# Who stores last, and when: the ends of four stages of a hybrid decoder step

## The reference, cut to what matters

```
proj = rms_norm(x) @ w_in            # columns of RWKV-7 (16 heads), then of NSA
rwkv_out = rwkv7_mix(token_shift(proj[:R_COLS]))         # head norm, bonus, gate at its end
q, cmp_kv, slc_kv, win_kv, gates = nsa_heads(proj[R_COLS:])
o_cmp, sel = cmp_attend_select(q, compress(cmp rows))    # top 16 of the 64-row blocks
o_slc = slc_attend(q, sel, slc_kv)   # the sampled tokens gather blocks from a paged cache
o_win = window_attend(q, win_kv)
x = x + concat(rwkv_out, gated sum of the three) @ w_o
x = x + (silu(h @ w_gate) * (h @ w_up)) @ w_down         # h = rms_norm(x)
return rms_norm(x), the new key and value rows, the new states
```

## Time and profile before

| | us |
|---|---|
| median of 3 runs | 3618.12 (3615.64 to 3628.66) |
| profiled execution | 3612.96 |
| its span | 3611.3 |

### The profile page before, as it was taken

One profiled execution on the slowest core, in us unless ns is written; L12 is line 12 of the kernel. 1 busy time (PEld: TensorE's weight loads), 2 busy tenths in 40 slices (PEclk: granted clock), 3 DMA queues, 4 the chain that ended last, 5 costly groups with the idle time before them and its releaser, 6 DMA issues. The chain is left out here.

```text
span 3611.3 us, 68792 instructions
## 1 busy us (share of the span) xinstructions
PE 3254.6 (90%) x28367; PEld 2980.1 (83%) x28367; DVE 1958.0 (54%) x2486; ACT 1210.8 (34%) x1824; POOL 523.4 (14%) x653
## 2 busy tenths in 40 slices
PE   6999997669977999858878978999999999999997
PEld 6999997348866778644436978999999999999997
DVE  4222221753335666326643237777777777777776
ACT  4111121532323655314412234333333333333333
POOL 2000000353433333444100000000000000000000
PEclk8999999579987999869988988999999999999999
DMA  7344431565545444355252222333333332333332
GB/s 219 107 117 116 110 102 45 185 184 140 131 122 198 186 186 151 119 144 140 54 178 62 83 69 76 106 94 100 106 94 106 96 109 89 101 109 94 106 93 96
DMA packets 491834, 426.27 MB, mean 118 GB/s; under 512 B 125749, under 2 KB 440614, under 8 KB 486942
## 3 DMA queue, kind: packets, MB, share of 16 engines
q1 hardware_dynamic: 470334, 300.38, 28.9%
q0 software_dynamic: 20736, 122.13, 9.7%
q10 hardware_dynamic: 512, 0.00, 0.0%
HBM read 382.96 MB, written 66.78 MB: 125 GB/s over the span
## 5 line engine op out<-in xcount | busy, mean ns | idle before, releaser
L2763 PE MATMUL d_ps<-f_t_hi,f_w_hi 128*128 128x260 f32 x2464 | 699.9, 284 | 39.7 <-DVE f_t_lo_r L3033 32.6
L2764 PE MATMUL d_ps<-f_t_lo_r,f_w_hi 128*128 128x260 f32 x2464 | 698.9, 284 | 0.0
L2763 PEld LDWEIGHTS d_ps<-f_t_hi,f_w_hi 128*128 128x128 f32 x2464 | 467.0, 190 | 40.5 <-issue 33.2
L2764 PEld LDWEIGHTS d_ps<-f_t_lo_r,f_w_hi 128*128 128x128 f32 x2464 | 467.4, 190 | 0.0
L2782 PE MATMUL d_ps<-f_hid_r,f_w_hi 128*128 128x260 f32 x2816 | 457.2, 283 | 0.0
L2825 ACT CAST f_w_hi<-f_raw 128x1024 fp32r<-128x1024 f32 x242 | 253.9, 1049 | 500.2 <-PE d_ps L2782 268.9
L2765 PE MATMUL d_ps<-f_t_hi,f_raw_r 128*128 128x260 f32 x1408 | 399.3, 284 | 0.0
L2782 PEld LDWEIGHTS d_ps<-f_hid_r,f_w_hi 128*128 128x128 f32 x2816 | 388.6, 188 | 0.0
L2905 DVE TENSOR_TENSOR f_raw_r<-f_raw,f_w_hi 128x1024 fp32r<-128x1024 f32 x242 | 295.9, 1223 | 50.0 <-ACT f_w_hi L2825 50.0
L53 PE MATMUL p_ps<-xh,p_w_hi 128*128 128x264 f32 (+2 forms) x1504 | 306.6, 285 | 10.6 <-DVE p_w_lo L306 10.6
L55 PE MATMUL p_ps<-xl,p_w_hi 128*128 128x264 f32 (+2 forms) x1504 | 306.1, 285 | 0.0
(11 more groups left out here) (483 smaller groups left out, 5883.1 us busy)
## 6 DMA issues: line engine op xcount, KB each, us to landing
p_w<-in_w_in SPq DMA_DIRECT2D x46, 1024.0 KB, 5.6
f_raw<-in_w_gate SPq DMA_DIRECT2D x88, 512.0 KB, 3.9
f_raw<-in_w_up SPq DMA_DIRECT2D x88, 512.0 KB, 3.9
f_raw<-in_w_down SPq DMA_DIRECT2D x66, 512.0 KB, 3.6
wo_raw<-in_w_o SPq DMA_DIRECT2D x16, 1024.0 KB, 5.4
f_sums<-in_w_down SPq DMA_DIRECT2D x22, 512.0 KB, 3.6
rk_chunks<-r_outb POOLq DMA_DIRECT2D x8, 1280.0 KB, 6.2
s_cur<-rk_chunks SPq DMA_DIRECT2D x8, 1280.0 KB, 7.2
```

Of the source, the lines that this page charges most:

```text
L2763: pe.matmul(out, w, xh, start=(m < 4 and k == 0), stop=False, skip_group_check=True)
L2764: pe.matmul(out, w, xl, start=False, stop=False, skip_group_check=True)
```

## The change

Five edits, all in what one engine issues and waits for; no arithmetic is added or removed.

1. Input projection: `store_rows` and `rows_out` move from GpSimd to SyncE. The gate rows and row block 0 are issued ahead of the weights of unit CU + 10 = 44, blocks 1 to 5 behind all weights; SyncE waits for them at the end, GpSimd for its column stores alone.
2. Head normalisation: SyncE does not wait for its eight stores; they count into a new semaphore `heads_stored`, which lives on. `mix_ahead` (GpSimd, prompt stage) and each `keep_blocks` (VectorE, compression) wait for all of them. `y_t` is allocated first of the RWKV arrays, so that it is `kc` that overlies it.
3. The second `compress_load` goes from the end of the head normalisation to the start of GpSimd's list in the compression.
4. Selection: SyncE runs `prompt_ahead` before it waits for the addresses, then stores them and waits for that store. The read of the row and the 26 gathers leave the stage; in the prompt stage SyncE gathers all four heads of token 0 too.
5. Prompt attention: the stores of quarters 2 and 3 move from GpSimd to SyncE, behind its gathers; there are four semaphores `mix_stored`, one for each quarter, and SyncE waits for all four at the end.

```diff
@@ input projection, SyncE
                 for u in range(UN):
                     s, n = u % 4, wide(u)
                     if u >= 4:
                         sp.wait_ge(lo_done, u - 3)
+                    if u == CU + 10:
+                        sp.wait_ge(row_copied, 2)
+                        store_rows(grow, g.gates, NG, gates_stored)
+                        rows_out(0)
                     sp.dma_start(w_raw[:, s, :, 0:n], w_view[:, :, cols(u)]).then_inc(loaded[s], 16)
+                for c in range(1, KU // 2):
+                    rows_out(c)
+                for b in range(2):
+                    sp.wait_ge(row_stored[b], 32 * (KU // 4))
+                sp.wait_ge(gates_stored, 32)
@@ input projection, GpSimd (store_rows and rows_out word for word to SyncE)
                 for u in range(UN):
                     columns_out(u)
-                    if u == GU + 2:
-                        pool.wait_ge(row_copied, 2)
-                        store_rows(grow, g.gates, NG, gates_stored)
-                    if u >= CU + 4 and (u - CU) % 2 == 0:
-                        rows_out((u - CU - 4) // 2)
-                rows_out(KU // 2 - 1)
                 for s in range(4):
                     pool.wait_ge(stored[s], stores_of(s, UN))
-                for b in range(2):
-                    pool.wait_ge(row_stored[b], 32 * (KU // 4))
-                pool.wait_ge(gates_stored, 32)
@@ head normalisation, SyncE, then GpSimd
                 for q in range(NPAIR):
                     sp.wait_ge(out_ready, q + 1)
-                    sp.dma_start(g.mix_t[q * P:(q + 1) * P, :], g.y_t[:, q, :]).then_inc(stored, 16)
-                sp.wait_ge(stored, 16 * NPAIR)
+                    sp.dma_start(g.mix_t[q * P:(q + 1) * P, :], g.y_t[:, q, :]).then_inc(g.heads_stored, 16)
...
                 pool.wait_ge(idx_ready, 1)
-                for h in range(2):
-                    compress_load(pool, g, h, h, h + 1)
+                compress_load(pool, g, 0, 0, 1)
@@ compression, GpSimd, then VectorE
+                compress_load(pool, g, 1, 1, 2)
                 arrange(0, 0, start=True)
                 refill(0, 0)
                 arrange(0, 1)
...
                 def keep_blocks(i):
                     dve.wait_ge(fin_done, i * F2 + 1)
+                    dve.wait_ge(g.heads_stored, 16 * NPAIR)
@@ selection, SyncE
-                with nc.allow_non_contiguous_dma(reason="small tables"):
-                    sp.wait_ge(adr_ready, 1)
-                    sp.dma_start(g.adr_d, adr[:]).then_inc(adr_out, 16)
-                    sp.wait_ge(adr_out, 16)
-                    sp.dma_start(adr_row[:].rearrange("o (m k) -> o m k", k=NS),
-                                 g.adr_d.rearrange("(m f) k -> f m k", f=4)[0:1]).then_inc(adr_in, 16)
-                sp.wait_ge(adr_in, 16)
                 prompt_ahead(sp, nc, g)
-                gather(sp, g, adr_row, regs, 0, (0, 1))
+                sp.wait_ge(adr_ready, 1)
+                sp.dma_start(g.adr_d, adr[:]).then_inc(adr_out, 16)
+                sp.wait_ge(adr_out, 16)
@@ prompt attention
-        mix_stored = [sem(f"mix_stored{s}") for s in range(2)]
+        mix_stored = [sem(f"mix_stored{i}") for i in range(4)]
...
+        def store(eng, i):
+            eng.wait_ge(o_kept, 4 * i + 4)
+            eng.dma_start(g.mix_t[D_R + i * 256:D_R + i * 256 + 256, 0:SEQ].rearrange("(g d) t -> d g t", d=C),
+                           mo[half(i), :, :]).then_inc(mix_stored[i], 16)
@@ prompt attention, SyncE, then GpSimd, then VectorE
-                gather(sp, g, adr_row, regs, 0, (2, 3))
-                for b in range(1, SP_TOKENS):
+                for b in range(SP_TOKENS):
                     if b == 3:
                         wo_ahead(sp, g)
                     gather(sp, g, adr_row, regs, b, range(4))
+                store(sp, 2)
+                store(sp, 3)
+                for i in range(4):
+                    sp.wait_ge(mix_stored[i], 16)
...
-                store(0)
+                store(pool, 0)
                 gather(pool, g, late_row, regs, SP_TOKENS + 2, range(2))
-                store(1)
+                store(pool, 1)
                 gather(pool, g, late_row, regs, SP_TOKENS + 2, range(2, 4))
-                store(2)
-                store(3)
-                for s in range(2):
-                    pool.wait_ge(mix_stored[s], 32)
...
                     if i >= 2 and t == 0:
-                        dve.wait_ge(mix_stored[i % 2], 16)
+                        dve.wait_ge(mix_stored[i - 2], 16)
@@ mix_ahead, called by GpSimd in the prompt stage
 def mix_ahead(pool, g):
+    pool.wait_ge(g.heads_stored, 16 * NPAIR)
     for q in range(4):
         mix_load(pool, g, q)
```

More of the change, by code:

```diff
@@ L335, in _, with store_rows, rows_out @@
             def _(sp):
+                def store_rows(src, dst, n, sem_):
+                    sp.dma_start(dst[0:SEQ].rearrange("(t p) n -> p t n", p=P), src[:, 0:4, 0:n]).then_inc(sem_, 16)
+                    sp.dma_start(dst[SEQ:TC], src[0:NB, 4, 0:n]).then_inc(sem_, 16)
+                def rows_out(c):
+                    sp.wait_ge(row_copied, 2 * c + 3)
+                    store_rows(orow[:, c % 2], g.kv_rows[:, c * 256:(c + 1) * 256], 256, row_stored[c % 2])
                 for u in range(UN):
@@ L399, in _ @@
             def _(pool):
-                def store_rows(src, dst, n, sem_):
-                    pool.dma_start(dst[0:SEQ].rearrange("(t p) n -> p t n", p=P), src[:, 0:4, 0:n]).then_inc(sem_, 16)
-                    pool.dma_start(dst[SEQ:TC], src[0:NB, 4, 0:n]).then_inc(sem_, 16)
                 def columns_out(u):
@@ L411, in columns_out @@
                         pool.dma_start(g.k_t[r:r + P, :], ob[:, s, 0:SEQ]).then_inc(stored[s], 16)
-                def rows_out(c):
-                    pool.wait_ge(row_copied, 2 * c + 3)
-                    store_rows(orow[:, c % 2], g.kv_rows[:, c * 256:(c + 1) * 256], 256, row_stored[c % 2])
                 for u in range(UN):
                     columns_out(u)
-                    if u == GU + 2:
-                        pool.wait_ge(row_copied, 2)
-                        store_rows(grow, g.gates, NG, gates_stored)
-                    if u >= CU + 4 and (u - CU) % 2 == 0:
-                        rows_out((u - CU - 4) // 2)
-                rows_out(KU // 2 - 1)
                 for s in range(4):
                     pool.wait_ge(stored[s], stores_of(s, UN))
-                for b in range(2):
-                    pool.wait_ge(row_stored[b], 32 * (KU // 4))
-                pool.wait_ge(gates_stored, 32)
 class Arrays:
@@ L1187, in stage_rwkv_post @@
             "bonus_ready", "rec_ready", "spread_done", "spread_read"))
-        chain, out_ready, stored = new_sem(nc, g, "e_chain"), new_sem(nc, g, "e_out_ready"), new_sem(nc, g, "e_stored")
+        chain, out_ready = new_sem(nc, g, "e_chain"), new_sem(nc, g, "e_out_ready")
         iota_ready, idx_ready = new_sem(nc, g, "e_iota_ready"), new_sem(nc, g, "e_idx_ready")
@@ L1721, in stage_nsa_select @@
         adr = sb("adr", [P, NS], I32)
-        adr_row = sb("adr_row", [1, NB * 4 * NS], I32)
         pt_row = sb("pt_row", [1, NB, 2], I32)
@@ L2233, in _ @@
                 pool.tensor_copy(causal_r[:], causal[:]).then_inc(masks_ready, 1)
-                def store(i):
-                    pool.wait_ge(o_kept, 4 * i + 4)
-                    pool.dma_start(g.mix_t[D_R + i * 256:D_R + i * 256 + 256, 0:SEQ].rearrange("(g d) t -> d g t", d=C),
-                                   mo[half(i), :, :]).then_inc(mix_stored[i % 2], 16)
                 clear_old(pool, g)
@@ L3278, in compress_ahead @@
     g.m_pt_in, g.m_w_in, g.m_idc_ready = (nc.alloc_semaphore("m_" + n) for n in ("pt_in", "w_in", "idc_ready"))
+    g.heads_stored = nc.alloc_semaphore("heads_stored")
     g.b_q_in = nc.alloc_semaphore("b_q_in")
@@ L3286, in sb @@
             return ctx.enter_context(nc.sbuf_tensor(name, shape, F32))
+        g.y_t = sb("y_t", [P, NPAIR, TC])
         g.gate_t = sb("gate_t", [P, NPAIR, TC])
         g.bonus_t = sb("bonus_t", [P, NPAIR, TC])
-        g.y_t = sb("y_t", [P, NPAIR, TC])
         g.chunk_decay = sb("chunk_decay", [P, NPAIR, SEQ // C])
```

## The result

The changed kernel took **3576.66 us** (median of 4 runs, 3572.64 to 3580.08) against 3617.16 (4 runs) for the kernel before: ratio 0.9881, 95% interval 0.9857 to 0.9905, so it is faster by about 1.2%. (A ratio here is worked out from all runs of a group; the two medians alone lie 40.5 us apart.) The forecast was 3578. The profiled execution took 3572.64 us, its span 3571.0.

A forecast was written before the change was run, and what follows sets the result against it. TensorE is busy for most of the span, but stage ends wait 51 us behind VectorE without arithmetic. Gains 4.7 + 7.5 + 2.4 + 14.9 + 10.3 = 39.8 us; 3618.12 - 39.8 = 3578 us, range 3567 to 3592.

The forecast's parts named there:

- The ends of the stages: Four stages end earlier: input projection by 4.7 us, head normalisation 7.5, selection 14.9, prompt attention 10.3.
- GpSimd's drain in the projection: Input projection: begins at the key store of unit 44, two units before the end, and is over before VectorE.
- the prediction's second part: End of the input projection: with SyncE storing rows, 617.1 against 621.8, gain 4.7 us, bounds 4 to 6.5.
- The drain behind one gather: End of head normalisation: GpSimd's drain takes half of 24.3 us, over by about 1083, so not late next.
- The start of the compression: Compression's start with the second gather ahead of the first copy: gain 2.4 us, bounds a loss of 2.2 and 4.
- The replay: Compression's start, one instruction at a time from the new barrier: first copy 3.8 to 7.4, ScalarE at 8.5 instead of 10.9.
- both 64x8 casts should pass between the copies: Compression's start: VectorE's two small casts get in between GpSimd's two copies, as in the preparation stage; ScalarE starts at 8.5.
- By that rule: Compression's start under a strict port lock: second cast waits 3.6 us more, ScalarE at 11.5, sum 36.8 instead of 39.8.
- The moved gather did not block GpSimd: Rival, compression's start: GpSimd's next copy waits for the gather's descriptors; 11.8 us lost, 3590; 8%.
- The drains went with GpSimd's own DMAs: Rival, projection and prompt ends: GpSimd's drain waits for all queues, following SyncE's stores; sum 26.4, 3592; 10%.
- SyncE did not become the prompt stage's bound: Rival, prompt attention: SyncE's 260 gathers decide from 1.03 us each; at 1.25 us 18 us slower, 3636; 3%.
- Each next stage followed its earlier barrier: Answers a rival: an end moves but the next stage's start doesn't follow; half of the gain, 3598; 6%.

The follow-up runs named there:

- part 3 undone: Changed kernel with both gathers back at the end of the head normalisation: 3582.81 us (5 runs), ratio 0.9897.
- part 2's: Kernel before, with only SyncE's wait for the head stores dropped, later waits added and y_t allocated first; both gathers stay: 3614.58 us, ratio 0.9987.
- parts 4 and 5 alone: Two kernels, each the kernel before with one edit: the selection's reordering (3603.53 us, ratio 0.9961); prompt quarters 2 and 3 stored by SyncE (3609.12 us, ratio 0.9975).
- parts 1, 4 and 5 alone: Besides the selection-only and prompt-store-only kernels: the kernel before with only the input projection's rows stored by SyncE, 3613.37 us, ratio 0.9986.

## Why the prediction was right, and where it was not

**The ends of the stages** were right in place and size: 4.9 us in the projection (forecast 4.7), 8.2 in the head stage (7.5), 14.0 in the selection (14.9), 9.1 in the prompt stage (10.3). What was off in them: SyncE's last store of the prompt stage took 4.6 us from VectorE's end to the barrier, not 3.6, since the 3.8 us of a 1 MB store had been made 3.3 for half the bytes, and the landing took 4.4 (median of SyncE's two); GpSimd's own stores of the same quarters, 4.2 us in the kernel before, were the nearer row. The address store landed 0.9 us later than forecast.

**GpSimd's drain in the projection** did not begin with the key store of unit 44, as the prediction's second part put it. GpSimd still waits for each unit's copy, the last one too, so it began at 611.4 and ended at 614.6, behind VectorE's 613.6. Only SyncE's landing, at 617.3, covered it. The term came out right; the reason for its cover was wrong. The drain behind one gather was 16.3 us, not half of 24.3; it ended 7 us before the stage did.

**The start of the compression** is the step that failed. The replay held up to GpSimd's first copy, which ended at 7.3 us (7.4 forecast). It had ScalarE at 8.5 us, because "both 64x8 casts should pass between the copies"; they did not. At this place VectorE and GpSimd took turns, a whole instruction each, in every profile: the second cast was issued 0.1 us after GpSimd's second copy had begun, and waited it out. The Trainium skill, page "SBUF — State Buffer", section "Who interferes with whom", says that the shared port pair is a lock held for a whole instruction. By that rule the prediction had ScalarE at 11.5; it was 11.0, and moving the casts gave 9.2 and 5.2, where turns had it at 8.7 and 5.2. The earlier trace rows had been read too far: there VectorE's second copy began at 679.88, 0.02 us ahead of GpSimd's next instruction; here the cast began behind it. The one that began first went first both times; no run tried this by itself.

**The 2.4 us of this step came nearly all the same**, by another way: ScalarE's ninth cast was 2.3 us ahead of the kernel before, 2.1 ahead of the kernel with part 3 undone, because TensorE's clock was back at 2.4 GHz when ScalarE started. The clock came back at 10.4 to 11.0 us in all five profiles with the changed kernel's compression. In the six with both gathers in the head stage it came back at 16.3 to 18.1 us, but in part 2's, which had it from 8.6 to 12.0 and again from 15.4 us on. Why it comes back sooner with the moved gather was not tried by itself. Over the whole stage the five took 399.1 us on the mean and the six 401.1, with single ones of the six from 395.8 to 404.2.

**What the sum left out** is the clock elsewhere. The chunk stage took 275.8, 272.3 and 269.2 us in three profiles whose kernels are the same up to it (before, parts 4 and 5 alone), and 269.2, 277.3 and 273.9 in the three of the changed kernel; the five profiles of its edited versions, which are the same up to there, range from 271.4 to 277.8, so the first profile was the lowest of eight. The compression took 395.8 us in the profile of before, but 404.2, 402.3 and 401.2 with parts 1, 4 and 5 alone, which leave it as it was, and 399.8, 399.6 and 398.4 with the change: the profile of before lay low there and high in the chunks. In the first pair of profiles +6.6 us in the chunks and -6.3 in the compression (a lead of 2.3 turned into a loss of 4.0) nearly cancelled. So the sum's closeness to a microsecond is luck; its four ends are not. That the three groups of the changed kernel had medians of 3576.7, 3574.2 and 3585.6 us is more than the chunk stage alone explains, and stays open.

**The parts add up, within the intervals.** Their ratios alone make 5.1, 4.7, 14.1 and 9.0 us, 32.9 together, and part 3 another 2.2 in the head stage and 2.1 at the start of the compression, 37 in all; the whole made 43 (34 to 52) by its ratio, and 47 and 33 in the other two groups.

**The rivals.** The moved gather did not block GpSimd: its first copy starts as the gather's instruction ends (1080.24 and 1.13, then 1081.37). The drains went with GpSimd's own DMAs (16.3 us behind one gather, 24.3 behind two) and not with SyncE's stores. SyncE did not become the prompt stage's bound: its last gather was issued at 1778.3, 30 us ahead of VectorE's end. Each next stage followed its earlier barrier.

## What to carry to other kernels

Read a stage's end by who is last there and what its last instruction waits for; a store or a drain behind the last arithmetic can be moved to the engine that has nothing else to drain, or its wait to the first reader, and ask each time what is late next: here first a drain 3 us behind VectorE, then a landing. An order that was changed for the right reason may still stand wrong in itself: the store that ends the stage belongs ahead of the loads that don't. Where two engines hold each other up, replay their queues one instruction at a time, and don't bank a microsecond of earlier start before seeing what it meets.

## What was not expected of the hardware

GpSimd's drain at the end of these four stages lasts 3.2 to 24.5 us once its list is through, and doesn't wait for the transfers of other queues: with part 5 alone it was over 73 us before SyncE's last store had landed. SyncE's issue of the address store stood for 4.73 us behind the twelve loads, where the same instruction took 0.58 us ahead of them. And a stage that nobody touched, at a granted clock of 0.94 to 0.98, differs by 8.6 us between profiles (269.2 to 277.8), more than most of the terms that were forecast.
